# First layer of a four-layer encoder trunk: another layout and order for the value weights, squares of x ahead of one split, one warm-up matmul fewer

## What is computed

```python
def _rmsnorm(x, g):
    y = xf * lax.rsqrt(jnp.mean(xf * xf, axis=-1, keepdims=True) + RMS_EPS)
    return (y * g.astype(jnp.float32)).astype(x.dtype)

def stick_breaking_mixer(h, w_qkv, w_o):        # h = rmsnorm(x, attn_norm[0])
    qkv = (h @ w_qkv).reshape(b, s, 3, SB_HEADS, SB_HEAD_DIM)
    q, k, v = qkv[:, :, 0], qkv[:, :, 1], qkv[:, :, 2]
    ...                                          # attention over q, k, v per head
    return _from_blocks(o).reshape(b, s, SB_HEADS * SB_HEAD_DIM) @ w_o
```

## Time and profile before

| | before |
|---|---|
| three runs | 1164.01, 1164.64, 1165.12 us |
| profiled execution, its own time | 1163.93 us |
| its span (first to last instruction) | 1162.1 us |
| TensorE busy | 1150.4 us, 99% of the span |
| VectorE, ScalarE, GpSimd busy | 803.2, 633.8, 275.8 us |
| mean granted TensorE clock | 0.998 |
| DMA engines busy, first of 40 slices | 0.9 |

### The profile page before, as it was taken

How to read it: one execution, slowest core, us unless ns; L and a number is a source line. 1 busy time by engine, 2 the same in 40 slices (tenths; PEclk the granted TensorE clock), 3 DMA queues, 4 the chain that set the end, 5 groups by cost and what they waited for, 6 DMA issues and landing times.

```text
span 1162.1 us, 17765 instructions
## 1 busy us (share of the span) xinstructions
PE 1150.4 (99%) x7208; PEld 1023.7 (88%) x7208; DVE 803.2 (69%) x880; ACT 633.8 (55%) x753; POOL 275.8 (24%) x257
## 2 busy tenths in 40 slices
PE   9999999999999999999999999999999999999997
PEld 7899888888998888888899888888889998888886
DVE  5776877776588677767657777767646868777742
ACT  6776565564355456555335656555446765655632
POOL 2100533231123444221111344221110005322100
PEclk9999999999999999999999999999999999999999
DMA  9432655565563355555554355555555326555550
GB/s 348 167 109 73 220 194 200 184 203 191 192 199 108 109 181 181 189 197 194 182 181 137 118 182 183 191 198 189 181 183 178 112 73 218 186 196 198 195 186 37
DMA packets 31227, 201.75 MB, mean 174 GB/s; under 512 B 3648, under 2 KB 4736, under 8 KB 7728
## 3 DMA queue, kind: packets, MB, share of 16 engines
q1 hardware_dynamic: 28800, 196.88, 48.0%
q10 hardware_dynamic: 2032, 3.07, 1.0%
q0 software_dynamic: 320, 0.72, 0.3%
HBM read 198.43 MB, written 1.25 MB: 172 GB/s over the span
## 4 chain that ended last, share of the span: by engine, by line
PE 96%; DMA 1%; DVE 1%; POOL 1%; SPq 1%; issue 1%; ACT 0%; ACTq 0%; DVEq 0%; POOLq 0%
PE banks L1335 41%; PE banks L1339 21%; PE banks L1323 8%; PE banks L1329 6%; PE banks L1331 6%; PE banks L1330 6%; PE banks L1470 1%; DMA raw<-w 1%; PE banks L1407 1%; PE banks L1484 1%; PE banks L1626 1%; PE banks L1653 1%; PE banks L1638 1%; PE banks L1472 0%; SPq L320 0%
## 5 line engine op out<-in xcount | busy, mean ns | idle before, releaser
L862 DVE TENSOR_TENSOR w_lo<-raw,w_hi 128x2048 fp32r<-128x2048 f32 x180 | 441.8, 2458 | 192.7 <-ACT w_hi L503 192.5
L503 ACT ACTIVATE w_hi<-raw 128x2048 fp32r<-128x2048 f32 x183 | 348.6, 1907 | 59.5 <-PE banks L1323 25.2
L1335 PE MATMUL banks<-x_split,w_hi 128*128 128x512 f32 x1408 | 336.9, 391 | 0.0
L1335 PEld LDWEIGHTS banks<-x_split,w_hi 128*128 128x128 f32 x1408 | 258.5, 188 | 50.2 <-DVE w_lo L862 0.4
L1339 PEld LDWEIGHTS banks<-x_split,w_lo 128*128 128x128 f32 x1408 | 181.0, 191 | 7.1
L1339 PE MATMUL banks<-x_split,w_lo 128*128 128x256 f32 x1408 | 184.0, 283 | 0.0
L1335 PE MATMUL banks<-hid_split,w_hi 128*128 128x512 f32 x528 | 129.9, 392 | 0.0
L1335 PEld LDWEIGHTS banks<-hid_split,w_hi 128*128 128x128 f32 x528 | 95.6, 188 | 17.4
L1329 PE MATMUL banks<-x_split,w_hi 128*128 128x256 f32 x384 | 110.0, 287 | 0.0
L1331 PE MATMUL banks<-x_split,w_lo 128*128 128x256 f32 x384 | 108.6, 283 | 0.0
L1330 PE MATMUL banks<-x_split,w_hi 128*128 128x256 f32 x384 | 108.6, 283 | 0.0
(11 more groups left out here) (199 smaller groups left out, 1637.0 us busy)
## 6 DMA issues: line engine op xcount, KB each, us to landing
raw<-w SPq DMA_DIRECT2D x183, 1024.0 KB, 4.9
raw<-w SPq DMA_DIRECT2D x8, 256.0 KB, 6.3
x<-x_in SPq DMA_DIRECT2D x4, 256.0 KB, 5.5
raw<-w SPq DMA_DIRECT2D x2, 512.0 KB, 7.5
k_all<-k_all ACTq DMA_DIRECT2D x1, 960.0 KB, 8.0
rel_bias<-rel_scratch POOLq DMA_DIRECT2D x8, 64.0 KB, 3.3
y_gain<-final_rows ACTq DMA_DIRECT2D x1, 512.0 KB, 6.3
out<-y_rows SPq DMA_DIRECT2D x2, 256.0 KB, 2.6
```

What stands on the lines that cost most here:

```text
L503: act.activation(w_hi[u % HI_SLOTS][:, :], raw[slot][:, :], ACT.Copy).then_inc(hi_done, 1)
L862: dve.tensor_tensor(w_lo[slot][:, :], raw[slot][:, :], w_hi[u % HI_SLOTS][:, :].bitcast(FP32), ALU.subtract).then_inc(lo_done, 1)
L1335: return pe.matmul(pair(b), wt[0], xs, start=first, stop=False, skip_group_check=True)
```

## The change

Five edits, all for layer 0 or the start of the program:

- The host lays out the value weights of layer 0 so that a unit holds two tiles k with all 1024 columns: left half and right half for k = 0, then for k = 1, and so on. PE walks them in that order, so each x tile gets both halves of the columns in turn, into the same four accumulator banks. The number of matmuls is the same.
- SP issues x pair 0, pieces 0 to 3, x pair 1, pieces 4 and 5, x pair 2, pieces 6 and 7, x pair 3, pieces 8 and 9, then the constants. Before, it was each x pair with two pieces, the constants, then pieces 8 and 9.
- ACT and DVE split two pieces per x tile for the first four tiles, then tiles 4 and 5, pieces 8 and 9, tiles 6 and 7.
- ACT squares x ahead of the split of unit 3, not behind it.
- The warm-up is six matmuls, not seven. The first half of the values is read from its banks after unit 3 (`unit_used` 4), not after unit 1.

```diff
-WARM_UP = 7
+WARM_UP = 6
...
-            for j in range(PAIRS):
+            for j, pieces in enumerate((range(0, 4), range(4, 6), range(6, 8), range(8, 10))):
                 sp.dma_start(x[:, 2 * j:2 * j + 2, :], x_in[:, 2 * j:2 * j + 2, :]).then_inc(x_loaded[j], 16)
-                piece(2 * j)
-                piece(2 * j + 1)
+                for i in pieces:
+                    piece(i)
             sp.dma_start(table[:, 0:C_KSUM], consts[:, 0:C_KSUM]).then_inc(one_loaded, 16)
-            for i in range(8, 10):
-                piece(i)
...
                 m, b, n = mixer[i], MIXER_BASE[i], 2 * i
-                split(b + (4 if i else 3))
                 if i == 0:
                     for j in range(PAIRS):
                         act.activation(first_squares[:, j, :], out_pair(j).rearrange("p a s -> p (a s)"),
                                        ACT.Square).then_inc(input_squared, 1)
+                split(b + (4 if i else 3))
+                if i == 0:
                     split(b + 4)
                     split(b + 5)
                     split(b + 6)
                 first_guess(norm, n + 1, 0, SEQ + TOKEN_SUMS[n])
-                value_half(m, b + 2, n, 0)
+                value_half(m, b + (2 if i else 4), n, 0)
...
                 norm_hi(0, k)
-                split_piece(k)
-            split_piece(8)
-            split_piece(9)
+                if k < 4:
+                    split_piece(2 * k)
+                    split_piece(2 * k + 1)
+                elif k == 5:
+                    split_piece(8)
+                    split_piece(9)
...
+                def value_product(u, at, kk, half):
+                    for t in range(2):
+                        xt = tuple(v[:, kk, t * P:(t + 1) * P] for v in (x_hi, x_lo))
+                        last = moving_weights(bank[SB_V_BANKS[half][t]][:, :], w_tile(u, at, 512), xt, kk == 0,
+                                              kk == KT - 1)
+                    return last
+
+                if i == 0:
+                    for u in range(4):
+                        for at in range(4):
+                            kk, half = 2 * u + at // 2, at % 2
+                            if u < 2 and at < 3:
+                                pe.wait_ge(piece_lo, 3 * u + at + 1)
+                            elif u == 2 and at == 0:
+                                pe.wait_ge(piece_lo, 7)
+                            elif (u < 2 and at == 3) or (u == 2 and at == 2) or (u == 3 and at == 0):
+                                pe.wait_ge(lo_done, u + 1)
+                            if half == 0:
+                                pe.wait_ge(norm.lo, kk + 1)
+                            last = value_product(u, at, kk, half)
+                        last.then_inc(unit_used, 1)
...
-            w[b:b + 4] = units(moving(qkv[:, 2 * D:], 512))
+            w[b:b + 4] = units(moving(qkv[:, 2 * D:], 512 if i else D))
```

More of the change, by code:

```diff
@@ L1413, in stick_breaking @@
                 m, b, n = mixer[i], MIXER_BASE[i], 2 * i
[L1414 to L1418, removed]
-                            pe.wait_ge(lo_done, u + 1)
[L1420 to L1440, removed]
@@ new lines, in value_product @@
+                def value_product(u, at, kk, half):
[18 more added lines that the diff above has]
+                        last.then_inc(unit_used, 1)
+                else:
+                    for half in range(2):
+                        for kq in range(2):
+                            u = b + 2 * half + kq
+                            pe.wait_ge(lo_done, u + 1)
+                            for k in range(4):
+                                if half == 0:
+                                    pe.wait_ge(norm.lo, 8 * n + 4 * kq + k + 1)
+                                last = value_product(u, k, 4 * kq + k, half)
+                            last.then_inc(unit_used, 1)
+                            if half == 0 and kq == 1:
+                                model_sums(n)
```

## The result

The changed kernel takes 1166.74 us, the median of 20 runs (1164.81 to 1167.38), against 1165.46 us for 20 runs of the kernel before (1164.01 to 1166.38): ratio 1.0013, 95% interval 1.0007 to 1.0019. The forecast was 1163.9 us, a little faster, with 1162.6 to 1166.0 for eight cases in ten. The sign and the range were wrong; the difference lies inside the 0.2% called "no change".

A forecast was written before the change was run, and what follows sets the result against it. PE was taken as the bound, busy 99%, with 2.56 us of pauses as ceiling. Those go and 1.6 to 1.7 come: -0.7 from 1163.93 gives 1163.2, as a median 1163.9 us, range 1162.6 to 1166.0.

The forecast's parts named there:

- Part 1: PE's waits at 9.45 (0.57 us) and 17.63 (0.15 us) for split weights would go, with piece 9 taken at 15.89.
- the fourth one: Rival at the start: piece 8 or x loads late, PE waits earlier, less at unit 3, same end; no separate chance.
- Part 2: At unit 3: squares start at 17.9, ACT's split at 19.98, DVE's at 21.91; unit 3 ready 0.95 us later.
- Part 3: DVE's split of unit 3 and POOL's third add collide within 0.06 us; DVE taken to go first, ready at 24.20.
- outcome (b): At unit 3 POOL gets the port first, costing DVE 1.09 us; ready at 25.3, sum +0.35; chance 0.30.
- My 0.15: The first 0.15 us of a POOL add seems to need no port, so DVE would still go first at unit 3.
- Part 4: The 1.45 us wait for POOL at the sums of squares goes; sums start at 31.3, 0.65 us sooner.
- Part 5: At the start: the two passes taken out come behind the clock's rise, PE waits 0.43 us longer; worth nothing.
- The clock: Rival: the clock falls in the pause at unit 3, matmuls behind it run at 1.2 GHz and lose 1.6; chance 0.07.

The follow-up runs named there:

- Batch 2: Changed kernel run again, full-clock median 1165.39 us, beside the changed kernel with its loads in the order of before, full-clock median 1164.13 us.
- two-and-two placement: Squares of pairs 0 and 1 ahead of unit 3's split, the others behind: 0.9983 in the kernel before, 0.9989 in the changed one, 0.9985 with old loads.
- old-load run: Changed kernel with the loads in the order of before, all else as changed: 1164.54 us, ratio 1.0004 to the kernel before.
- both repairs: Changed kernel with the squares spread over ACT's idle times and the old load order: 1164.00 us with six warm-up matmuls, 1163.99 with seven.

## Why the prediction was wrong

**Part 1, the early pauses: half right.** The pause at 9.45 went as said. The step that failed is the reading of landings as a place in a line, one every 0.64 us whatever the order. In the new order the sixth load comes 1.1 us late, and all behind it: PE waits 1.15 for piece 4, x pair 1 and piece 4 being late, and piece 9 is taken at 16.99 against a forecast 15.89. Batch 2 put the price at 1.26 us of full-clock time (1165.39 against 1164.13). That is the price with all squares ahead; with the two-and-two placement it was 0.4. No rival held this; the fourth one named late loads but said "with the same end", which is refuted.

**Part 2, unit 3 behind the squares: right in mechanism, start shifted.** Squares to split 2.10 (forecast 2.08), split to DVE 1.93 (1.93). The start, 18.84 for 17.9, carries Part 1's lateness.

**Part 3, DVE against POOL: the wrong side was taken.** The starts lay 0.06 apart, as computed, and the first to start won: outcome (b), at its price, 3.38 - 2.29 = 1.09. My 0.15 of an add "that needs no port" was read off the ends of blocked adds, which say nothing of when the port is taken. In the old-load run DVE again took 6.13 for two splits that take 4.58 alone. The rule of the Trainium skill ("SBUF — State Buffer", "Who interferes with whom"), that issue order decides, agrees with these traces and gave the right answer; I had set it below a guess.

**Part 4, the sums: right in kind.** The wait at the sums went. It went also because PE came 2.8 us later.

**Part 5, the warm-up: right in price, wrong in its reading of the clock, and so by luck.** Worth nothing in two comparisons (0.9999; 0.9991 against 0.9992). But the two passes were not taken from behind the rise: the twelve passes of the changed kernel last 4.47 us, the fourteen of before 4.48, since weight loads of 0.34 us, at the low level, go on until 5.04 there and until 4.19 before. The rise differs between executions, with seven matmuls too: 0.34 us at 6.32 in the profile of both repairs with seven.

**The clock: a rival with 0.07 that decided 15 of 20 runs.** Its place (unit 3) and its price (1.6) were right; it cost 1.41 in the profile, and the two groups of runs lie 1.2 to 1.9 us apart in the kernels above. I held the one pause of 1.45 us without a fall in the profile of before against it. A single trace could not carry that: the kernel before itself falls in a quarter of its runs. Where it falls there was not traced; that none of the 33 runs with two and two fell speaks for the wait at the sums. The pauses ahead of unit 3 were 2.4 to 2.9 us in the four profiles where the clock fell, and two of 2.6 and 3.4 passed without. The page "TensorE: Matmul & The Clock Gate" of the Trainium skill, section "What's actually happening", says that idleness gates the clock, and the four profiles agree.

Together, for the profiled pair: predicted -0.7, measured +2.8. The gap is late loads (18.84 against 17.9, 0.95), the port (1.1) and the clock (1.4): -0.7 + 0.95 + 1.1 + 1.4 = 2.75.

Over the runs the shares differ. The changed kernel's full-clock median, 1165.53, lies inside the range of 1162.6 to 1166.0: the falls took the time out of the range. The sign was wrong without them: the full-clock medians of the kernel before are 1164.1 to 1164.5. And 0.8 of the 2.8 us between 1163.9 and 1166.74 is the base: I counted from 1164.64, the median of three runs of before, and 20 runs have 1165.46.

At full clock, each kernel against the before of its own batch, the squares ahead alone cost 0.77; with all the rest of the change but its load order the loss is 0.02; with the load order too it is 1.28. So the gain that Part 1 forecast at the early pauses (0.57 + 0.15) seems to be there, 0.75. It pays for the moved squares, and the load order undoes it. No run had the layout alone.

## What to carry to other kernels

When a sum of small terms rests on a pause of PE, price the clock with it, and ask how often in many runs, not whether in one trace; the mean granted clock of each run tells. When work for two engines that share a port is forecast to start within a tenth of a microsecond, take the order that the forecast gives if both hang on the same instruction, as here, and else plan for the worse one; or move half of the work away, as the two-and-two placement did. Shorten the wait that is there (POOL late at the sums) by feeding it just early enough; moving all of it ahead made the wait for unit 3 out of the wait for the sums.

## What the runs showed of the hardware

- The order of 256 KB loads changes when they land, not only which comes first: the sixth load, issued at 3.09 in all, landed 5.7 to 6.1 us later in the old order, 7.0 to 8.0 in the new one. The cause was not found.
- Matmuls of a zero tile into an unused bank kept the granted clock up through the pause, in 22 of 22 runs by their mean clock, with no cost to the matmuls behind (they end 0.35 us ahead of unit 3 in the profile).
- DVE's SCALAR_TENSOR_TENSOR with two inputs in SBUF is held by a POOL add like its TENSOR_TENSOR: two took 2.60 us beside POOL and 0.88 alone.
- The length of a pause alone does not decide on the fall. With both repairs the profiles have pauses of 2.06 and 1.64 us near 19.6, and none of the 33 runs fell. The kernel before, with 1.62 ahead of the weight load of the sums as its longest, has the fall in 34 of 132 runs.
- The median of the 20 runs of the kernel before, 1165.46, above the first three runs' 1164.64, may carry some falls; their clocks were not recorded.
